# Compressing the paged key and value cache as a two-tap filter in three products, in a one-layer decoder step

## The reference, cut to what matters

```python
c = kv[:, :n_chunk * 16].reshape(B, n_chunk, 16, 2, N_KV_HEADS, 64)
lo = einsum('bnjchd,cjde->bnche', c, w1[:, :16])      # first tap
hi = einsum('bnjchd,cjde->bnche', c, w1[:, 16:])      # second tap
pre = lo[:, :-1] + hi[:, 1:] + pe_term[:, None, :]    # pe_term = position table times w1
return einsum('bnche,ced->bnchd', gelu(pre), w2)
```

## Time and profile before

| what | value |
|---|---|
| median of 3 runs | 1812.33 us (1809.98 to 1816.35) |
| the profiled execution | 1815.14 us |
| its span in the profile | 1813.5 us |
| mean granted TensorE clock | 0.994 of full speed |
| PE busy | 1758.8 us (97%) |
| PE weight loads busy | 1638.0 us (90%) |
| DVE / ACT / POOL busy | 1207.8 / 765.9 / 803.5 us |
| transfers | 214.60 MB, mean 118 GB/s |

### The profile page before, as it was taken

The page is one execution under the profiler, slowest core; times in us unless marked ns, Lnnn a source line. Parts: engine busy times, 40 slices in busy tenths (PEclk is TensorE's granted clock), DMA queues, the critical chain, the costliest instruction groups (busy, mean ns, idle before and its releaser), DMA issues.

```text
span 1813.5 us, 36969 instructions
## 1 busy us (share of the span) xinstructions
PE 1758.8 (97%) x14084; PEld 1638.0 (90%) x14084; DVE 1207.8 (67%) x1909; ACT 765.9 (42%) x1433; POOL 803.5 (44%) x763
## 2 busy tenths in 40 slices
PE   8999999999998999999999899999999999999998
PEld 7999999999995767676899799999999999999998
DVE  6789975676466677767646745455587879855535
ACT  5312333345345666666624333333343333314435
POOL 2203972224303434344444666655665545425531
PEclk9999999999998999999999999999999999999999
DMA  4321365436413444444313332333394633432214
GB/s 157 127 74 43 104 197 151 132 97 166 111 49 117 129 129 121 126 124 123 120 47 116 104 107 95 115 111 107 116 294 148 200 109 121 143 102 64 58 35 143
DMA packets 189983, 214.60 MB, mean 118 GB/s; under 512 B 23012, under 2 KB 152736, under 8 KB 189287
## 3 DMA queue, kind: packets, MB, share of 16 engines
q1 hardware_dynamic: 179357, 188.89, 33.8%
q0 software_dynamic: 7840, 21.25, 4.2%
q10 hardware_dynamic: 2610, 2.10, 0.4%
HBM read 181.22 MB, written 35.55 MB: 120 GB/s over the span
## 4 chain that ended last, share of the span: by engine, by line
PE 51%; DVE 9%; issue 3%; ACT 3%; POOL 2%; DMA 1%; ACTq 0%; SPq 0%; DVEq 0%; POOLq 0%
PE ps L2660 11%; PE ps L3043 6%; PE ps L2665 5%; PE ps L2420 5%; PE ps L3048 3%; PE ps L200 3%; PE ps L1827 3%; PE ps L1839 3%; PE ps L1815 3%; PE ps L3556 2%; POOL S L1782 2%; PE ps L1866 2%; PE ps L206 1%; DVE S L2076 1%; DVE dn_op_lo L3091 1%
## 5 line engine op out<-in xcount | busy, mean ns | idle before, releaser
L1782 POOL TENSOR_SCALAR S<-S,inv,gate_p 128x640 f32<-128x640 f32 (+7 forms) x186 | 124.8, 690 | 195.2 <-DVE inv L2086 195.2
L1166 DVE SCALAR_TENSOR_TENSOR y<-u,conv_w,y 128x1024 f32<-128x1024 f32 x120 | 156.5, 1350 | 1.2
L433 POOL DMA_DIRECT2D raw<-in_cache_cmp_kv_dram x124 | 77.8, 632 | 149.2 <-DVE relaid L1252 120.5
L1010 PE MATMUL ps_p<-Xhi,w1hi 128*128 128x256 f32 x544 | 139.3, 294 | 1.4 <-ACT Xhi L715 1.4
L3043 PE MATMUL ps<-dn_op_hi,dn_hi 128*128 128x264 f32 x672 | 136.7, 285 | 3.5 <-DVE dn_op_lo L3091 3.5
L3043 PE MATMUL ps<-dn_op_lo,dn_hi 128*128 128x264 f32 x672 | 135.7, 283 | 0.0
L1010 PE MATMUL ps_p<-Xlo,w1hi 128*128 128x256 f32 x544 | 132.9, 283 | 0.0
L1236 DVE TENSOR_TENSOR Xlo<-ps_p,Xhi 128x512 fp32r<-128x512 f32 x132 | 85.0, 685 | 59.3 <-ACT Xhi L715 59.2
L715 ACT ACTIVATE Xhi<-ps_p 128x512 fp32r<-128x512 f32 x132 | 72.4, 598 | 104.2 <-PE ps_p L935 96.8
L1963 ACT ACTIVATE S<-S,mn 128x64 f32<-128x64 f32 (+8 forms) x180 | 108.7, 608 | 2.1 <-DVE mn L2076 2.1
L3043 PEld LDWEIGHTS ps<-dn_op_hi,dn_hi 128*128 128x128 f32 x672 | 103.7, 188 | 4.9 <-DVE dn_op_lo L3091 4.8
(11 more groups left out here) (502 smaller groups left out, 4918.5 us busy)
## 6 DMA issues: line engine op xcount, KB each, us to landing
s_raw<-in_cache_slc_kv_dram SPq DMA_DIRECT2D x256, 128.0 KB, 2.1
dn_op_raw<-hidden SPq DMA_DIRECT2D x21, 1056.0 KB, 5.7
raw<-in_cache_cmp_kv_dram SPq DMA_DIRECT2D x132, 128.0 KB, 4.2
hidden<-cs SPq DMA_DIRECT2D x32, 528.0 KB, 2.6
up_raw<-in_w_up_dram SPq DMA_DIRECT2D x16, 1024.0 KB, 5.5
raw<-in_cache_cmp_kv_dram POOLq DMA_DIRECT2D x124, 128.0 KB, 4.5
dn_w<-in_w_down_dram SPq DMA_DIRECT2D x48, 256.0 KB, 5.2
win_raw<-in_w_in_dram SPq DMA_DIRECT2D x38, 256.0 KB, 3.3
```

What stands on the lines that cost most here:

```text
L1010: mm = nc.tensor.matmul(ps_h[n % 2][:, 0:w], ws[cc][:, j, :], x[n % 2][:, j % 8, slice(j // 8, j // 8 + w)], start=(j == 0 and m == 0), st ...
L1166: i = V_.scalar_tensor_tensor(out=y, in0=x, scalar=w, in1=y, op0=ALU.mult, op1=ALU.add)
L1782: nc.gpsimd.tensor_scalar(x, x, inv[:, n % 3, 3 * e + br:3 * e + br + 1], c.gate_p[:, i, H * br + h:H * br + h + 1], ALU.mult, ALU.mult).t ...
```

## The change

The two taps over an even and an odd chunk make two outputs, and these are computed from three products instead of four. With even and odd chunks x0, x1 and the next even chunk x2, taps a (first) and b (second):

- output 0 = a x0 + b x1 and output 1 = a x1 + b x2.
- The kernel after computes P0 = b x(even), P1 = a x(odd), and P2 = (a - b)(x(even) - x(odd)). Then output 0 = P0 + P1 + P2, and output 1 = P1 + P0 of the next even chunk.

P0 and P1 are the three rounded products as before; P2 is one plain float32 product with the difference tiles `w1diff`.

What moves:

- **Pages.** A page lands as 16 rows of 8 tokens, 8192 bytes each, on every eighth partition (q, q+8, ..., q+120). 32 pages, a whole sequence, make one buffer of 32 KB a partition; there are two. All are issued by SP (`load_pages`), four to a register load; for the first sequence in two halves that go through all register loads twice. Sequence b+1 is loaded when b-1 has been relaid. POOL issues no page. The prompt's own rows come as one transfer, and the position table as eight more rows, written by way of DRAM.
- **Steps.** `CPAIRS` has 18 entries (prompt keys, prompt values, then sequence x kind, both heads together), each of four steps; 72 steps. A step holds 4 of the 16 tokens of a chunk pair: 8 turns into two banks, a high part of 1024 columns and a 512-column copy on ACT, low part and difference (512) on DVE, 12 rounded and 2 plain products of 256 columns on PE. The turns of the step after next stand between the rounded and the plain products.
- **Relay** goes from DVE to POOL, two copies of 512 columns a step.
- **Combination.** After a pair, ACT copies the odd part out of PSUM (`odd`), DVE adds (`combine`, four instructions), ACT applies gelu, PE runs the second layer for both heads, and ACT keeps the result.
- **Banks.** The eight PSUM banks are dealt out anew; the norm's sums use a product bank between two pairs and its steps are spread over the steps of pairs 3 to 12. The tables on POOL are cut into eight parts between relays. The low half of the key weights is made after the last tap. The last rows are stored before the first page is loaded. The weights of the value half come in one load.

The diff, cut to its core:

```diff
-AUX = (... + [f"rows{r}" for r in range(NR)] + ["gate"])
+AUX = (... + [f"rows{r}" for r in range(NR)])
-NQD = NPG // 8
-UNITS = [(None, 0), (None, 1)] + [(b, ch) for b in range(B) for ch in range(4)]
+CPAIRS = [(None, 0), (None, 1)] + [(b, cc) for b in range(B) for cc in range(2)]
+NPAIR = len(CPAIRS)
+NST = 4 * NPAIR
...
+            def load_pages(b, quads):
+                for q in range(NPG // 4):
+                    _, at = nc.values_load_multi_w_load_instructions(
+                        c.pages[0:1, ds(b * NPG + 4 * q, 4)], engines=[mybir.EngineType.SP], min_val=0, max_val=N_POOL - 1)
+                    for g in quads:
+                        sp.dma_start(raw[b % 2][q:P:8, g, :], cs_rows[ds(at[g], 1)].rearrange("o x f -> (o x) f")).then_inc(raw_loaded[b % 2], 16)
...
+            sp.dma_start(raw[1][:, 2, :], cp_rows).then_inc(prompt_loaded, 16)
             store_rows(8)
+            sp.wait_ge(conv_step, conv_taps)
+            sp.wait_ge(s_new, CT)
+            sp.wait_ge(turned[1], aux("conv") + 1)
+            load_pages(0, (0, 1))
             spill_q(3)
-            for g in (2, 3, 4):
-                load_quad(sp, mybir.EngineType.SP, 0, g)
             sp.wait_ge(free[0], 10)
...
+            sp.wait_ge(W.done, NT)
+            load_pages(0, (2, 3))
...
+            for b in range(1, B):
+                sp.wait_ge(relaid_ready, 8 * b)
+                load_pages(b, range(4))
+            sp.wait_ge(relaid_ready, 8 * B)
             sp.dma_start(c.q[:].rearrange("p g r -> p (g r)"), q_dram).then_inc(c.q_back, 16)
...
+            def relay(st):                                        # on POOL
+                b, cc = CPAIRS[st // 4]
...
+                elif b is not None and cc == 0 and st % 4 == 0:
+                    pool.wait_ge(raw_loaded[b % 2], 16 * NPG * (b // 2 + 1))
+                if st >= 2:
+                    pool.wait_ge(chunks_turned, st - 1)
+                for h in range(KVH):
+                    out, src = relay_of(st, h)
...
+                        i = nc.gpsimd.tensor_copy(out, src)
+                i.then_inc(relaid_ready, 1)
...
+            def hi(st):                                           # on ACT
+                act.wait_ge(chunks_turned, st + 1)
...
+                i = nc.scalar.activation(split_columns(st, Xhi[st % 2]), turned_columns(st), ACT.Copy)
+                if st >= NST_PROMPT:
+                    after(act, used, st - NST_PROMPT - 1)
+                    i = nc.scalar.activation(split_columns(st, Xdiff[st % 2]), turned_columns(st)[:, 2:4], ACT.Copy)
+                i.then_inc(hi_ready, 1)
...
+            def layer1(st, following=None):                       # on PE
+                n, s = divmod(st, 4)
...
+                pe.wait_ge(lo_ready, st + 1)
+                halves, difference = ps_h[n % 2]
+                for k, j in enumerate(token_pairs(st)):
+                    for e, at in ((0, j + 8), (1, j)):
...
+                        nc.tensor.matmul(out, w1hi[cc][:, at, :], x_hi, start=first, stop=False)
+                        nc.tensor.matmul(out, w1hi[cc][:, at, :], x_lo, start=False, stop=False)
+                        mm = nc.tensor.matmul(out, w1lo[cc][:, at, :], x_hi, start=False, stop=last)
+                mm.then_inc(split_used, 1)
+                if following is not None:
+                    turn(following)
...
+                pe.wait_ge(diff_ready, st + 1 - NST_PROMPT)
+                for k, j in enumerate(token_pairs(st)):
+                    mm = nc.tensor.matmul(difference[:, 0:NC], w1diff[cc][:, j, :], Xdiff[v][:, k, :], start=(s == 0 and k == 0), stop=(s == 3 and k == 1))
+                mm.then_inc(used, 1)
...
+            turn(1)
+            for st in range(NST - 2):
+                n, s = divmod(st, 4)
+                layer1(st, st + 2)
...
+                norm(n, s)
+                if s == 1 and n:
+                    layer2(n - 1)
...
             first_scores_of(0)
+            layer1(NST - 2)
             first_scores_of(1)
+            layer1(NST - 1)
             first_scores_of(2)
+            layer2(NPAIR - 1)
...
+            def combine(n):                                       # on DVE
...
+                V_.tensor_tensor(even, p0, p1, ALU.add).then_inc(summed, 1)
+                V_.tensor_tensor(odd[:, :, 0:15, :], p0[:, :, 1:16, :], p1[:, :, 0:15, :], ALU.add)
...
+                V_.tensor_tensor(even, p2, even, ALU.add).then_inc(combined, 1)
```

More of the change, by code:

```diff
@@ L408, in both_read, with turned_columns, split_columns, relay_of @@
                 eng.wait_ge(read[half], aux(name) + 1)
[L410 to L433, removed]
+        def turned_columns(st):
+            if st < NST_PROMPT:
+                return ps_x[st % 2][:, :, 0:2 * PROMPT_W].rearrange("p h (n x) -> p x h n", x=2)
+            return ps_x[st % 2].rearrange("p h (m x n) -> p x (h m) n", x=4, n=8)
+        def split_columns(st, x):
+            if st < NST_PROMPT:
+                return x.rearrange("p x (h n) -> p x h n", h=KVH)[:, 0:2, :, 0:PROMPT_W]
+            return x.rearrange("p x (m n) -> p x m n", n=8)
+        def relay_of(st, h):
+            b, cc = CPAIRS[st // 4]
+            src, out = raw[1 if b is None else b % 2], relaid[st % 2]
+            if b is None:
+                src, out = src[:, 2:4, :], out[:, 0:2]
+            t = 2 * (st % 4)
+            src = src.rearrange("p g (t c h d) -> p g c h t d", t=HALF_T, c=2, h=KVH)[:, :, cc, h, t:t + 2, :]
+            return out[:, :, h, :].rearrange("p g (t d) -> p g t d", d=DH), src
         @block.sync
@@ L561, in _ @@
             send_x(0)
+            for cc in range(2):
+                for h in range(KVH):
+                    pool.dma_start(pe_dram[:, cc, h, :], a["pe_cmp"][0, cc]).then_inc(pe_spread, 16)
             pool.wait_ge(scaled, NR)
@@ L592, in _ @@
                 tap(k)
[L593 to L601, removed]
@@ L624, in _ @@
+            for st in range(NST):
+                n, s = divmod(st, 4)
+                relay(st)
+                if n in (TABLE_PAIR, TABLE_PAIR + 1):
+                    tables_part(4 * (n - TABLE_PAIR) + s)
         @block.scalar
@@ L811, in gelu @@
                     act.wait_ge(bias_kept, cc + 1)
-                nc.scalar.activation(hid[:, n % 2, 0:w], ps_h[n % 2][:, 0:w], ACT.Gelu_apprx_tanh,
-                                     bias=c.pe_bias[:, cc:cc + 1]).then_inc(gelu_done, 1)
-            def norm(n):
-                j, step = divmod(n - FIRST_NORM, 3)
-                if 0 <= j < NCH and step == 2:
+                    x, out = x[:, :, 0:64], hid[:, (n + 1) % 2, :, 0:64]
+                else:
+                    act.wait_ge(combined, n - 1)
+                    x = out = hid[:, (n + 1) % 2]
@@ L834, in first_exps @@
+            keep(NPAIR - 2)
             def first_exps(i, ch):
@@ L845, in _ @@
             first_exps(1, 0)
+            odd(NPAIR - 1)
+            gelu(NPAIR - 1)
             first_exps(1, 1)
-            gelu(NU - 1)
+            keep(NPAIR - 1)
         @block.tensor
@@ L1053, in _ @@
-            for n in range(NU):
-                for part in range(2):
-                    if n >= 2 or (n, part) == (1, 1):
-                        turn(n, part)
-                    if n:
-                        layer1(n - 1, part)
-                    if part == 0:
-                        norm(n)
-                if n == 1:
-                    pe.wait_ge(free[0], 10)
-                    begin(0, "gate")
-                    for r in range(QB):
-                        mm = nc.tensor.transpose(ps_a[:, 24 * r:24 * r + 24], gT[0:24, P * r:P * r + P], c.ident[0:24, 0:24])
-                    mm.then_inc(turned[0], 1)
-                if n >= 2:
-                    layer2(n - 2)
+                out = ps_h[n % 2][1]
@@ new lines, in layer2 @@
+                for h in range(KVH):
+                    if b is None and cc == 0:
+                        mm = nc.tensor.matmul(out[DH * h:DH * h + DH, NC:NC + 64], w2[:, 0, :], hid[:, (n + 1) % 2, h, 0:64], start=True, stop=True)
+                    elif b is None:
+                        mm = nc.tensor.matmul(out[0:64, NC + DH * h:NC + DH * h + DH], hid[:, (n + 1) % 2, h, 0:64], w2[:, 1, :], start=True, stop=True)
+                    elif cc == 0:
+                        mm = nc.tensor.matmul(out[DH * h:DH * h + DH, NC:2 * NC], w2[:, 0, :], hid[:, (n + 1) % 2, h, :], start=True, stop=True)
+                    else:
+                        for f in range(NC // P):
+                            at = NC + P * f + DH * h
+                            mm = nc.tensor.matmul(out[:, at:at + DH], hid[:, (n + 1) % 2, h, P * f:P * f + P], w2[:, 1, :], start=True, stop=True)
@@ L1411, in _ @@
             first_scores_of(1)
+            combine(NPAIR - 1)
             dve.wait_ge(first_exp, 6)
```

639 lines of the change are left out of this document (316 added, 323 removed).

## The result

The kernel after takes **1843.91 us** (median of 4 runs, 1842.39 to 1845.54) against 1813.17 (1809.98 to 1816.35) of the kernel before beside it: ratio **1.017, 95% interval 1.0148 to 1.0191**, 31 us slower. The forecast was 1828, with a range that ended at 1842. In the profiled executions it is 1842.39 against 1815.14: 27 us where the sum had 15.6. The direction and the place were right, and the sum had half the size. Every median here is of executions in the chip's fast state; run 2 alone had one in the slow state (3362.74 us), and its median is given without it.

The account below looks back on a forecast made before the run. SyncE's page issues were to bound the compression stage, 31.9 us a sequence against PE's 26.6; with late entry, seven further sequences and the tail it ends at 562.8 instead of 547.2, so 1812.3 + 15.6 = 1828 us, range 1786 to 1842.

Parts of the forecast that it names:

- What bounds it: Compression stage: SyncE's page issues become the bound, 31.9 us a sequence against 26.6 of PE, by 5.3 us.
- PE's step: Sampled steps on PE: 12 rounded products, 8 turns, 2 plain products (0.86) make 3.15 us; eight steps are 25.2.
- The issue of a page: Page loads on SyncE: 0.656 us a page, 3.99 a group of four, 31.9 a sequence.
- the entry: Stage start: first-sequence halves 21.3 us each, prompt steps hidden by 290, sampled products from 301, further sequences issued from 294.6.
- the last part: Stage end: last page landed at 520.0, then last steps, query reload and a 5.5 us tail, ending at 562.8.
- The reload of the queries: Near stage end: cannot start before the last relay at 541.8, takes 9.1 us, PE idle for some 3.
- The relay: GpSimd's two strided copies of 512 columns a step: bounds 1.5 to 2.7 us, taken as 1.6, hidden by a step.
- B: Rival: 16-row page issue as cheap as the 128-row one, 0.52 us a page; 22 us faster, 1790 us; chance 0.20.
- C: Rival: page issue still cheaper, 0.45 us, PE bound; 28 us faster, 1784 us; chance 0.09.
- D: Rival: page issue dearer, 0.78 us, 256 pages adding 32 us more, 1860 us; chance 0.06.
- E: Rival: VectorE, ScalarE or GpSimd binds, 19 us on top of C (1803); chance 0.07 on top of B or C.
- The switch: Page pitch on SyncE dividing faster from slower: stage end 547 at about 0.60 us a page.

Follow-up runs that it names:

- run 2: Kernel after with pages read from fixed addresses in order, no page table or register work (other values computed): 1785.16 us, ratio 0.9858 to before.
- run 1: Kernel after with the range check of page numbers on SyncE taken out: 1787.53 us, ratio 0.987 to before.
- run 3: Kernel after with GpSimd issuing 8 of the 32 pages of every sequence but the first, checks kept: 1802.68 us, ratio 0.9946 to before.
- run 9: Kernel after with the range check taken out of every second group of four pages: 1805.09 us, ratio 0.9962.
- run 10: Kernel after with one more register load and range check per group of four pages, value unused: 1886.04 us, ratio 1.04.
- run 6: Kernel after, checks kept, each page landing as 128 rows of 1024 bytes over all partitions (other values computed): 1799.39 us, ratio 0.9924 to before.

## Why the prediction was right in kind and wrong in size

- **What bounds it: right.** SyncE's issues bind, PE stands before nearly every eighth step, put down to the relay and behind it to the page, with the clock at half for some us. Shown by runs 1, 3, 9 and 10.
- **PE's step: right.** 3.17 us for 3.15 (turns at 339.70, 342.86, 346.03). The make-up was off, with a plain product at 0.34 for my 0.43 and a seam of 0.19 where the kinds change, and cancelled. A sequence of PE is 27.03 for 26.6: the second layer costs 0.9 in its step and 0.8 at the seam. The stalls of the norm (5.2 us in all) were not in the sum at all; hidden behind the loads in the kernel after, they show in run 1.
- **The issue of a page: the step that failed, as the mis-sized term "a page 0.656, a group of four 3.99".** It measured 4.26, and over 56 groups that is 14.9 us. With the 4 of the entry, less the 2.4 of the last part (both below), these are the 16 by which the stage ended later than forecast (578.95 for 562.8). Two parts. Uninterrupted, a group takes 4.10: 16 rows are issued in 0.496 us and not the 0.469 of 64 rows; 0.11. The other 0.15 are interruptions: eight of the 224 issues took 1.0 to 1.4 us (5.7 us over the usual), and nine pauses of 0.35 come some 26 us apart. The trace says more of both than I had seen: between two pauses lie exactly 128 instructions of SyncE, register work included, here and in every other run that I counted (before, 1, 6, 9, 10), and each of the eight long issues begins within 0.4 us behind the start of a transfer of 16 KB that the profile puts down to instructions:

```profile
q8 instruction: 12, 0.20, 0.3%
q14 instruction: 14, 0.11, 0.2%
```

So a range check costs its own time and brings the next pause nearer. That the transfers cause the long issues is likely by their times, but no run shows it. Both kinds were in the trace before. My own row had the maximum of 1635 ns beside the median, but that issue was the last of its burst, behind the last start that I counted; and the sixteen issues at 306 took 15.4 us from first to last where mine took 13.9. Of the six bursts of sixteen only one other took 13.9, and I read one of these two as if it were the mean:

```profile
L433 SPq DMA_DIRECT2D raw<-in_cache_cmp_kv_dram x16: 468/469/1549, 305.9 to 321.3; - x16
```

- **The entry: 4 us short.** SyncE began with the first half at 248.8 (forecast 249.0). The halves took 23.1 and 22.6 us for 21.3, the same error as above; spill, gate writes and gate reads took 4.0 for 3.0. The register work of the second sequence began at 298.5, its first page went out at 300.0, where the sum had 296.0. The gate writes have a price that I didn't see: they are queued behind the first half of the pages, VectorE waits 9.2 us for them, and PE stands 7.1. It runs the rest of the prompt's steps at half clock, as it does in run 1 without that stand. I had called these steps hidden by 290; all but the last ended at 292, still ahead of the pages.

```profile
276.43 0.36 DVE L1423 COPY gate_p<-ps_p 128x192 f32<-128x192 f32 x1 [9.18 <-DMA gates_sampled<-gT]
```

- **The reload of the queries: wrong, and without weight.** I had it wait for the last relay (issued 541.8, PE idle 3 us). The diff lets it go earlier: it writes over the buffer of the even sequences alone and was issued at 536.5, right behind the last page, and landed 20 us ahead of its reader. The 3 us were not there; from the landing of the last page to the end of the stage it took 40.4 for my 42.8.
- **The relay: 1.17 us a step for 1.6**, two copies of 0.6; the low end of my bounds was still too high.
- **The rivals.** B and C asked for a cheap issue. Run 6 has B's issue (0.333) and took 1799.4 us, not 1790: its group was 3.61 and not 3.44, by the same interruptions. Run 1 has C's group (3.18 for 3.16) and took 1787.5 for 1784. That is near in part by luck: its sampled products began at 289.7 and not 295, and its seven sequences took 198.3 us (284.83 to 483.12) and not 190: 9.1 of it are the norm's work and waits, for 3.5 in C. D had the right sign for the wrong reason: no dearer registers, but interruptions. E did not show. The switch, put at a pitch of 0.60 a page, is a group of 3.77; between run 9 (mean group 3.67, 1805) and the kernel after (4.26, 1844), 1813 lies at about 3.8.

## What to carry to other kernels

Take the time of a repeated issue from the longest unbroken stretch, first start to last start over the count, and look at the maximum beside the median: an engine that is about to bind pays its interruptions in full. When loads move to one queue, sum its instructions' time and not its bytes, with the pauses that their number brings: here 256 issues with their checks outlasted the products they feed, and two register instructions a page were worth 56 us. Before a change that takes work off the bounding engine, write down for each other engine how much of the period it will fill; a margin of minus 5 us in 27 was visible, and either of two small edits (a check less, a quarter on another queue) turns the loss into a gain. Another shape of the rows did so in time as well (run 6), but it puts the tokens in other places, and a kernel that works with them there was not built.

## What the runs showed of the hardware that I had not expected

- For a page of 128 KB with its address in a register, the issue time on SyncE falls as the rows grow in number: 16 rows 0.496 us, 64 rows 0.469, 128 rows 0.333. The Trainium skill ("Perfetto Trace Analysis", What "DMA-bound" means) advises large descriptors also where the issuing sequencer is the bound; run 6 went the other way, with rows of 1024 bytes 44 us faster than with 8192.
- A fixed address makes the 16-row issue slower, 0.589 against 0.496 (run 2). The 0.590 of the earlier trace rows, which I had taken for the price of 16 rows, is that of a fixed address.
- SyncE pauses 0.35 us after every 128 instructions of its own (runs before, after, 1, 6, 9, 10): every 26.1 us in the kernel after, every 22.0 in run 6, where the issues are shorter. Why, no run shows.
- A register load of four page numbers took 0.297 us, and 0.33 to the next instruction; the slowest, first behind a wait, 0.572. The Trainium skill ("DMA: Bandwidth & Descriptors", Latency and other measured facts) has some 600 ns as its floor; the trace doesn't agree.
- In run 1 the clock is at half from 270.3 to 287.4 although PE is busy nearly throughout (16.0 us of 16.0 in 272 to 288) and had only stood 0.84 us at 262 and 0.15 at 270.3; it was running the prompt's steps, products of 132 columns. Half clock isn't tied to a long stand here. What ties it, no run here shows.
